# A gated-linear-attention recurrence on one NeuronCore: scores with exchanged operands in four column groups, and the small matmuls of a step in one block

## Chip, cores and metric

The kernel runs on one core of a Trainium2 chip. The metric is the device time of one launch in microseconds (us). The profile is of one execution; engines are named PE (TensorE matmuls), PEld (its weight loads), DVE (VectorE), ACT (ScalarE), POOL (GpSimd) and SP (the queue that issues the transfers).

## The reference, cut to what matters

Two layers run over 1024 prompt rows and 64 sample rows (8 sequences of 8). The second layer is gated linear attention with 4 heads, and the change lies in its recurrence:

```python
bcum = jnp.cumsum(lg, axis=3); blast = bcum[:, :, :, -1:]
q_dec   = q * jnp.exp(bcum)
k_intra = k * jnp.exp(-bcum)
k_state = k * jnp.exp(blast - bcum)
att = jnp.where(causal, jnp.einsum('nbhid,nbhjd->nbhij', q_dec, k_intra), 0.0)
o_intra = jnp.einsum('nbhij,nbhje->nbhie', att, v)
...
    o_inter = jnp.einsum('bhid,bhde->bhie', qc, s)
    s = dc[..., None] * s + jnp.einsum('bhjd,bhje->bhde', kc, vc)
```

Each head's output is then normalised, multiplied by a SiLU gate (`z`) and projected. The sample rows do the same with a state of their own, loaded and stored per sequence.

## The kernel before

Large products (`product_step`, the matmuls at L515) are made of a high and a low part: three passes (`w_hi` by `h_hi`, `w_hi` by `h_lo`, `w_lo` by `h_hi`) of three matmuls each, so nine matmuls per 128 rows of the contraction. Weights arrive in `stage` by SP, ACT copies the high part (`split_slot`, L317), POOL subtracts for the low part (`lo_slots`, L322).

The GLA layer loops over 4 heads. A head projects q, k, decay and v, turns v, runs the recurrence, and then the gate piece Z3, the row norms (NRM) and the output products. The gate pieces Z0, Z1 and Z2 (8 product steps each, 24 in all) are cut up by `fill(n)` and laid between the small matmuls of the recurrence, so that PE has work while the other engines prepare operands. `FILL_START` and `FILL_STEP` set how many stand before the loop and in each step.

The recurrence takes 128 prompt rows a step, 8 steps, and the loop has two more turns since the sample work trails by two. All engines are written out by hand and meet by semaphores. On PE, step `s` of the kernel before is:

- a fill of one product step; `scores(s+1)` (L1756, four matmuls with the 128 columns of `Kp[:, b]` stationary and 32 columns of `qd` moving, into `X[0]`); `key_rows(s+1)` (L1766, a transpose); `output(s)` (L1774 with the scores, L1782 with the state `S`); `update(s)` (L1791, the state's new term into `ps[1][:, 2]`)
- a fill of one product step; `mean_square(s-1)` (L1846, waits for POOL's `square_sum`); every second step `sample_inter` (L1811, waits for two sample states); `sample_update(s-2)` (L1823, L1824; waits for `ksm` of DVE's `ks_rows`)

After the loop's last turns come `sample_out` (L1833, L1838) and the last `sample_update`, then Z3. ACT in step `s` has: `gate_in` in steps 0 and 4 (the SiLU of a finished gate piece, which needs another activation table than Exp, L1140); `ksT_out(s+1)`; `exps(s+2)` (L1098 to L1105: `Kp`, `qd`, `ks`); `o_out(s)` (square and copy of the output); `exp_qs(s+1)`; `split_slot` in steps 1 and 5. POOL has `scale_kp(s+2)` (L881, `Kp` times the keys, without which no scores can start), `lo_slots` in steps 1 and 5, and `square_sum(s)` (L890, L892). DVE masks the scores into `att` (`att_out`, L1398, two buffers), scales `qd`, `ks`, `qs`, keeps the state (`state`, L1410), and has `ks_rows` (L1417, L1418) and `sample_state` (L1424) of the samples. SP loads a sample state into the place of the v rows that `update(s)` has read (`load_state`, L726).

Of the kernel before, what the change touches and what calls it, by code (L numbers as in the profile page):

```python
# [24 lines left out]
P = 128  # L25
# [5 lines left out]
KG = GW // P  # L31
TP = 1024
NB = 8
# [32 lines left out]

FILL_START, FILL_STEP = 7, 2

MINIS = 11

# [20 lines left out]
def trunk(nc, x_prompt, x_sample, c_prompt, c_sample, state_pool, state_gla, ada_w, ada_b, norm_g,  # L91
# [8 lines left out]
    with ctx:  # L100
# [128 lines left out]
        def sem(name):  # L229
            return ctx.enter_context(nc.semaphore(name))  # L230
# [43 lines left out]
        kp_zero, kp_exp, kp_ready = sem("kp_zero"), sem("kp_exp"), sem("kp_ready")  # L274
        qd_arg, qd_exp, qd_ready = sem("qd_arg"), sem("qd_exp"), sem("qd_ready")
        qs_exp, qs_ready, ks_exp, ks_ready = sem("qs_exp"), sem("qs_ready"), sem("ks_exp"), sem("ks_ready")
        att_done, att_ready, o_done, o_evac = sem("att_done"), sem("att_ready"), sem("o_done"), sem("o_evac")
        kT_done, ksT_ready, upd_done, S_ready = sem("kT_done"), sem("ksT_ready"), sem("upd_done"), sem("S_ready")
        smp_arg, smp_exp, smp_ready = sem("smp_arg"), sem("smp_exp"), sem("smp_ready")
# [636 lines left out]
        def _(act):  # L916
# [125 lines left out]
            def head(g, first):  # L1042
# [65 lines left out]
                def exp_qs(s):  # L1108
                    if s >= 1:
                        act.wait_ge(o_done, g * NSUP + s)  # L1110
                    nc.scalar.activation(qs[:], L[:, s * SUP:(s + 1) * SUP], ACT.Exp).then_inc(qs_exp, 1)

                def ksT_out(s):
                    act.wait_ge(kT_done, g * NSUP + s + 1)
                    if s >= 2:
                        act.wait_ge(upd_done, g * NSUP + s - 1)
                    nc.scalar.activation(ksT[:, s % 2, :], ps[1][:, 1, 0:P], ACT.Copy).then_inc(ksT_ready, 1)
# [31 lines left out]
                exp_qs(0)  # L1149
                act.wait_ge(smp_kT, g + 1)  # L1150
                nc.scalar.activation(ksT_s[:], ps[1][:, 1, 0:P], ACT.Copy).then_inc(smp_ksT, 1)
                ksT_out(0)
                exps(1)
                for s in range(NSUP):
                    if s in (0, 4):
                        gate_in(s // 4)
                    if s + 1 < NSUP:
                        ksT_out(s + 1)
                    if s + 2 < NSUP:
                        exps(s + 2)  # L1160
                    o_out(s)
                    if s + 1 < NSUP:
                        exp_qs(s + 1)
                    if s in (1, 5):
                        split_slot(L1, GP, act, g, GP.slot["Z2"] + s // 4)
                gate_in(2)
                act.wait_ge(smp_rows_done, g + 1)
                nc.scalar.activation(smp_rows, X[1], ACT.Copy).then_inc(smp_rows_out, 1)
                split_slot(L1, GP, act, g, GP.slot["O01"])
                o_out(NSUP)  # L1170

# [38 lines left out]
        def _(dve):  # L1210
# [134 lines left out]
            with dve.Fori(0, NG) as g:  # L1345
# [46 lines left out]

                def att_out(s):

                    if s >= 2:
                        wait_apart(dve, o_done, g * NSUP + s - 1)
                    wait_apart(dve, att_done, g * NSUP + s + 1)
                    nc.vector.copy_predicated(att[:, s % 2, :], causal[:], X[0][:, 0:P])\  # L1398
                        .then_inc(att_ready, 1)

                def state(s):
# [68 lines left out]
                qd_args(1)  # L1470
                scale_qk(1)
                for s in range(NSUP + 2):
                    if s >= 2:
                        ks_rows(s - 2)
                    if s + 1 < NSUP:
                        att_out(s + 1)
                    if s + 2 < NSUP:
                        qd_args(s + 2)
                        scale_qk(s + 2)
                    if s < NSUP:  # L1480
                        state(s)
                    if s + 1 < NSUP:
                        scale_qs(s + 1)
                    if s >= 2:
                        sample_state(s - 2)

                dve.wait_ge(s0_ready, (g + 1) * NB)
                dve.wait_ge(o_evac, (g + 1) * NSUP)
# [40 lines left out]
        def _(pe):  # L1529
# [179 lines left out]
            def head(g, first):  # L1709
# [38 lines left out]
                def scores(s):  # L1748
                    pe.wait_ge(kp_ready, g * NSUP + s + 1)
                    pe.wait_ge(qd_ready, g * NSUP + s + 1)  # L1750
                    if s >= 1:
                        pe.wait_ge(att_ready, g * NSUP + s)
                    else:
                        pe.wait_ge(smp_attr, g + 1)
                    for b in range(4):
                        last = nc.tensor.matmul(X[0][:, b * CH:(b + 1) * CH], Kp[:, b, :], qd[:, b * CH:(b + 1) * CH],  # L1756
                                                start=True, stop=True)
                    last.then_inc(att_done, 1)

                def key_rows(s):  # L1760
                    pe.wait_ge(ks_ready, g * NSUP + s + 1)
# [6 lines left out]
                def output(s):  # L1768
# [3 lines left out]
                        pe.wait_ge(o_evac, g * NSUP + s)  # L1772
                    for e in range(KG):
                        last = nc.tensor.matmul(ps[1][:, 0, e * P:(e + 1) * P], v[:, s, e * P:(e + 1) * P],  # L1774
                                                att[:, s % 2, :], start=(e == 0), stop=(s == 0 and e == KG - 1),
                                                skip_group_check=True)
                    if s:
                        pe.wait_ge(S_ready, g * NSUP + s)
# [7 lines left out]
                def update(s):  # L1786

                    pe.wait_ge(ksT_ready, g * NSUP + s + 1)
                    if s >= 3:
                        pe.wait_ge(s0_ready, g * NB + s - 2)  # L1790
                    nc.tensor.matmul(ps[1][:, 2, :], ksT[:, s % 2, :], v[:, s, :], start=True,  # L1791
                                     stop=True).then_inc(upd_done, 1)

# [22 lines left out]
                def sample_update(b):  # L1816

                    pe.wait_ge(ksm_ready, g * NB + b + 1)
                    if b + 2 < NSUP:
                        pe.wait_ge(S_ready, g * NSUP + b + 3)  # L1820
                    else:
                        pe.wait_ge(s0_ready, g * NB + b)
                    nc.tensor.matmul(ps[1][:, 2, :], ksm[:, 0, :], v_s[:], start=True, stop=False)  # L1823
                    nc.tensor.matmul(ps[1][:, 2, :], ksm[:, 1, :], v_s[:], start=False,  # L1824
                                     stop=True).then_inc(smp_upd, 1)
# [39 lines left out]
                fill(1)  # L1865
                scores(0)
                key_rows(0)
                fill(FILL_START - 5)
                for s in range(NSUP + 2):
                    if s <= NSUP:  # L1870
                        fill(1)
                    if s + 1 < NSUP:
                        scores(s + 1)
                        key_rows(s + 1)
                    if s < NSUP:
                        output(s)
                        update(s)
                        fill(FILL_STEP - 1)
                    if 1 <= s <= NSUP:
                        pe.wait_ge(att_ready, g * NSUP + min(s + 2, NSUP))  # L1880
                        mean_square(s - 1)
                    if s in (2, 4, 6, 8):
                        sample_inter(s - 2)
                    if s == NSUP + 1:
                        sample_out()
                    if s >= 2:
                        sample_update(s - 2)
                pe.sem_inc(L1.unit_done, 1)

                u = GP.unit["Z3"]  # L1890
# [61 lines left out]
```

## Time and profile before

| | us |
|---|---|
| median of 3 runs | 1720.27 |
| lowest and highest | 1717.53, 1724.99 |
| the profiled execution | 1722.27 |
| its span, first to last instruction | 1720.5 |
| PE busy | 1644.9 (96%) |
| DVE, ACT, POOL busy | 833.3, 483.5, 397.3 |
| mean granted TensorE clock | 0.98 of full speed |

The span is 1.8 us below the execution's own time, and that execution is 2.0 us above the median. A busy PE is not PE at its peak: ends of matmuls are modelled. The chain of waits counts each piece from the end of the one before it, so its durations add up to time.

### The profile page before, as it was taken

What the parts mean: (1) busy time and instruction counts of PE and PEld (TensorE: products, weight loads), DVE (VectorE), ACT (ScalarE), POOL (GpSimd) and SP (SyncE); (2) the same over time, 40 slices, a digit from 0 to 9 for tenths busy, and PEclk for the clock granted to TensorE, in tenths of its full rate; (3) what the DMA queues carried; (4) which work ended last, traced back from release to release, by engine and by line L of the source; (5) the groups of instructions that cost most, each with busy time, mean ns of one, the idle gap of its engine ahead of it and who ended that gap; (6) DMA issues with size and microseconds to landing.
All of it is one profiled execution on the core that took longest, in us unless ns stands there. A gap on an engine that the chain in (4) does not pass through costs nothing.

```text
span 1720.5 us, 26408 instructions
## 1 busy us (share of the span) xinstructions
PE 1644.9 (96%) x10307; PEld 1564.1 (91%) x10307; DVE 833.3 (48%) x1245; ACT 483.5 (28%) x1021; POOL 397.3 (23%) x392
## 2 busy tenths in 40 slices
PE   6899999999999999997999999999999999999997
PEld 3798999999999999996898899988999889998896
DVE  4494439453844475456224561235621456324465
ACT  4321112110211111134335403264132532225423
POOL 3221212121221212113224121232112331213310
PEclk8999999999999999997999999999999999999999
DMA  9322211221222122210112211122111221111212
GB/s 352 129 62 72 75 44 55 74 76 39 67 76 62 53 66 71 67 27 26 37 38 75 80 39 50 37 62 80 51 38 37 62 92 38 41 47 38 98 43 104
DMA packets 145621, 115.23 MB, mean 67 GB/s; under 512 B 5885, under 2 KB 128345, under 8 KB 145506
## 3 DMA queue, kind: packets, MB, share of 16 engines
q1 hardware_dynamic: 143680, 112.87, 21.3%
q8 instruction: 91, 1.49, 0.4%
q10 hardware_dynamic: 1834, 0.74, 0.2%
q14 instruction: 16, 0.13, 0.0%
HBM read 99.05 MB, written 15.00 MB: 66 GB/s over the span
## 4 chain that ended last, share of the span: by engine, by line
PE 88%; DVE 8%; ACT 2%; issue 1%; DMA 1%; SPq 0%; POOL 0%; ACTq 0%; DVEq 0%
PE psA L515 45%; PE psB L515 29%; PE psB L1774 2%; PE psB L1791 2%; PE psX L1756 2%; DVE PQ L1273 2%; PE psB L1782 1%; PE psX L1811 1%; DMA ada<-in_ada_w 1%; PE psB L1823 1%; DVE y_rows L1523 1%; PE psX L1636 1%; DVE a_hi L591 1%; ACT PQ L1049 1%; DVE ksm L1418 1%
## 5 line engine op out<-in xcount | busy, mean ns | idle before, releaser
L322 POOL TENSOR_TENSOR w_lo<-stage,w_hi 128x1024 fp32r<-128x1024 f32 x112 | 279.0, 2492 | 1059.4 <-ACT w_hi L317 1059.4
L515 PE MATMUL psA<-h_hi,w_hi 128*128 128x362 f32 (+1 forms) x1152 | 277.4, 350 | 24.5 <-DVE h_lo L453 15.3
L515 PE MATMUL psA<-h_lo,w_hi 128*128 128x362 f32 (+1 forms) x1152 | 256.9, 332 | 0.0
L515 PE MATMUL psA<-h_hi,w_lo 128*128 128x362 f32 (+1 forms) x1152 | 255.6, 330 | 0.0
L515 PEld LDWEIGHTS psA<-h_hi,w_hi 128*128 128x128 f32 x1152 | 202.4, 192 | 53.5 <-issue 48.3
L317 ACT ACTIVATE w_hi<-stage 128x1024 fp32r<-128x1024 f32 x112 | 120.1, 1072 | 392.3 <-PE psB L515 301.3
L515 PEld LDWEIGHTS psA<-h_lo,w_hi 128*128 128x128 f32 x1152 | 204.2, 193 | 0.0
L515 PEld LDWEIGHTS psA<-h_hi,w_lo 128*128 128x128 f32 x1152 | 203.4, 192 | 0.0
L515 PE MATMUL psB<-h_hi,w_hi 128*128 128x362 f32 (+1 forms) x576 | 129.1, 332 | 1.7 <-ACT kT L1049 1.7
L515 PE MATMUL psB<-h_hi,w_lo 128*128 128x362 f32 (+1 forms) x576 | 126.3, 327 | 0.0
L515 PE MATMUL psB<-h_lo,w_hi 128*128 128x362 f32 (+1 forms) x576 | 126.2, 327 | 0.0
L515 PE MATMUL psA<-a_hi,w_hi 128*128 128x362 f32 (+1 forms) x480 | 108.2, 333 | 5.9 <-DVE a_lo L594 5.9
L515 PE MATMUL psB<-a_hi,w_hi 128*128 128x362 f32 (+1 forms) x480 | 106.0, 329 | 4.2 <-DVE a_lo L1294 4.2
L515 PE MATMUL psA<-a_lo,w_hi 128*128 128x362 f32 (+1 forms) x480 | 105.7, 328 | 0.0
L515 PE MATMUL psB<-a_hi,w_lo 128*128 128x362 f32 (+1 forms) x480 | 105.6, 328 | 0.0
L515 PE MATMUL psA<-a_hi,w_lo 128*128 128x362 f32 (+1 forms) x480 | 105.3, 327 | 0.0
L515 PE MATMUL psB<-a_lo,w_hi 128*128 128x362 f32 (+1 forms) x480 | 105.3, 327 | 0.0
L515 PEld LDWEIGHTS psB<-h_hi,w_hi 128*128 128x128 f32 x576 | 98.3, 189 | 7.4 <-issue 6.3
L1273 DVE SCALAR_TENSOR_TENSOR PQ<-PQ,win_on 128x1220 f32<-128x1220 f32 (+2 forms) x48 | 103.2, 2150 | 2.8 <-DVE PQ L1268 0.5
L515 PEld LDWEIGHTS psB<-h_hi,w_lo 128*128 128x128 f32 x576 | 99.9, 188 | 0.0
L515 PEld LDWEIGHTS psB<-h_lo,w_hi 128*128 128x128 f32 x576 | 99.8, 188 | 0.0
L1364 DVE COPY v<-psB 128x512 f32<-128x512 f32 x32 | 20.6, 686 | 150.2 <-PE psB L1719 150.2
(314 smaller groups left out, 2369.7 us busy)
## 6 DMA issues: line engine op xcount, KB each, us to landing
stage<-in_gla_w_in SPq DMA_DIRECT2D x40, 512.0 KB, 3.9
stage<-in_pool_w_in SPq DMA_DIRECT2D x32, 512.0 KB, 4.1
ada_stage<-in_ada_w SPq DMA_DIRECT2D x24, 512.0 KB, 3.5
ada<-in_ada_w SPq DMA_DIRECT2D x8, 1024.0 KB, 12.2
stage<-in_pool_w_out SPq DMA_DIRECT2D x16, 512.0 KB, 3.5
v<-in_state_gla SPq DMA_DIRECT2D x32, 256.0 KB, 2.6
out_new_gla_sample<-v SPq DMA_DIRECT2D x32, 256.0 KB, 2.1
stage<-in_gla_w_out SPq DMA_DIRECT2D x16, 512.0 KB, 3.6
```

The source lines that it names most:

```text
L317: nc.scalar.activation(w_hi[:, j % 2, :], stage[:, j % 2, :], ACT.Copy).then_inc(lay.hi_done, 1)
L322: nc.gpsimd.tensor_tensor(w_lo[:, j % 2, :], stage[:, j % 2, :], w_hi[:, j % 2, :].bitcast(f32), ALU.subtract).then_inc(lay.lo_done, 1)
L515: last = nc.tensor.matmul(ps[u][:, t, 0:width], weight(w[:, p, :], k), a[:, k, n0:n0 + width], start=(k == 0 and pas == 0), stop=(k == kt ...
L591: nc.vector.tensor_copy(a_hi[:, i, :], oT[:, i, :]).then_inc(chain_v, 1)
L1049: last = nc.scalar.activation(dst[:, n0:n0 + w], ps[GP.set[u]][:, t, 0:w], ACT.Copy, scale=scale)
L1273: link(nc.vector.scalar_tensor_tensor(out=dst[:, lo:WE], in0=src[:, lo - sh:WE - sh], scalar=win_on[:].rearrange("p g k -> p (g k)")[:, ds ...
L1364: nc.vector.tensor_copy(v[:, 4 * half:4 * half + 4, i * P:(i + 1) * P], ps[1][:, half, :].rearrange("p (s n) -> p s n", s=4))
L1418: nc.vector.scalar_tensor_tensor(out=ksm[:, 1, :], in0=ksT_s[:], scalar=seq_rows[:, b:b + 1], in1=ksm[:, 0, :].bitcast(f32), op0=ALU.mult, ...
L1523: nc.vector.scalar_tensor_tensor(out=y_rows[0:n, s, :], in0=ps_y[s % 3][0:n].rearrange("p a n -> p (a n)"), scalar=y_rms[0:n, s:s + 1], in ...
L1756: last = nc.tensor.matmul(X[0][:, b * CH:(b + 1) * CH], Kp[:, b, :], qd[:, b * CH:(b + 1) * CH], start=True, stop=True)
L1774: last = nc.tensor.matmul(ps[1][:, 0, e * P:(e + 1) * P], v[:, s, e * P:(e + 1) * P], att[:, s % 2, :], start=(e == 0), stop=(s == 0 and e ...
L1791: nc.tensor.matmul(ps[1][:, 2, :], ksT[:, s % 2, :], v[:, s, :], start=True, stop=True).then_inc(upd_done, 1)
```

## The change

The scores' operands are exchanged: the 32 columns of `qd` of block `b` become the stationary operand and the 128 columns of `Kp[:, b]` the moving one, and the result of block `b` lies in partitions 32b to 32b+31 of `X[0]`, so each matmul uses another group of 32 columns of the array. The result is queries by keys, while `output` wants keys by queries. So ACT copies it to `att[:, 1]` (`scores_out`), PE turns it back into `X[0]` (`turn_scores`), and DVE masks it from there. `att` has one buffer left for the masked scores.

The order in the step is rewritten on PE, ACT and DVE, as the diff shows. PE has one block of small matmuls and then both product steps of fill; one product step moves from the start into the loop. `gate_in` moves from steps 0, 4 to 1, 5; the third one moves behind the copy of the sample rows. `update(s)` now waits for the `sample_state` of its own step.

```diff
-FILL_START, FILL_STEP = 7, 2
+FILL_START, FILL_STEP = 6, 2
+                def scores_out(s):
+                    act.wait_ge(att_done, g * NSUP + s + 1)
+                    if s >= 1:
+                        act.wait_ge(turn_done, g * NSUP + s)
+                    nc.scalar.activation(att[:, 1, :], X[0][:, 0:P], ACT.Copy).then_inc(score_out, 1)
...
+                scores_out(0)
                 ksT_out(0)
                 exps(1)
                 for s in range(NSUP):
-                    if s in (0, 4):
+                    if s + 1 < NSUP:
+                        scores_out(s + 1)
+                    if s in (1, 5):
                         gate_in(s // 4)
...
-                gate_in(2)
                 act.wait_ge(smp_rows_done, g + 1)
                 nc.scalar.activation(smp_rows, X[1], ACT.Copy).then_inc(smp_rows_out, 1)
+                gate_in(2)
...
-                    if s >= 2:
-                        wait_apart(dve, o_done, g * NSUP + s - 1)
-                    wait_apart(dve, att_done, g * NSUP + s + 1)
-                    nc.vector.copy_predicated(att[:, s % 2, :], causal[:], X[0][:, 0:P])\
+                    if s >= 1:
+                        wait_apart(dve, o_done, g * NSUP + s)
+                    wait_apart(dve, turn_done, g * NSUP + s + 1)
+                    nc.vector.copy_predicated(att[:, 0, :], causal[:], X[0][:, 0:P])\
...
                 for s in range(NSUP + 2):
+                    if s + 2 < NSUP:
+                        qd_args(s + 2)
                     if s >= 2:
-                        ks_rows(s - 2)
+                        sample_state(s - 2)
                     if s + 1 < NSUP:
                         att_out(s + 1)
                     if s + 2 < NSUP:
-                        qd_args(s + 2)
                         scale_qk(s + 2)
...
-                    if s >= 2:
-                        sample_state(s - 2)
+                    if 1 <= s <= NSUP:
+                        ks_rows(s - 1)
...
-                        last = nc.tensor.matmul(X[0][:, b * CH:(b + 1) * CH], Kp[:, b, :], qd[:, b * CH:(b + 1) * CH],
+                        last = nc.tensor.matmul(X[0][b * CH:(b + 1) * CH, 0:P], qd[:, b * CH:(b + 1) * CH], Kp[:, b, :],
...
+                def turn_scores(s):
+                    pe.wait_ge(score_out, g * NSUP + s + 1)
+                    nc.tensor.transpose(X[0][:, 0:P], att[:, 1, :], ident[:]).then_inc(turn_done, 1)
...
-                    if s >= 3:
-                        pe.wait_ge(s0_ready, g * NB + s - 2)
+                    if s >= 2:
+                        pe.wait_ge(s0_ready, g * NB + s - 1)
...
-                    if b + 2 < NSUP:
-                        pe.wait_ge(S_ready, g * NSUP + b + 3)
+                    if b + 2 <= NSUP:
+                        pe.wait_ge(S_ready, g * NSUP + b + 2)
...
                 fill(1)
                 scores(0)
                 key_rows(0)
+                turn_scores(0)
                 fill(FILL_START - 5)
                 for s in range(NSUP + 2):
-                    if s <= NSUP:
-                        fill(1)
                     if s + 1 < NSUP:
                         scores(s + 1)
                         key_rows(s + 1)
+                    if s in (2, 4, 6, 8):
+                        sample_inter(s - 2)
+                    if s >= 2:
+                        sample_update(s - 2)
                     if s < NSUP:
                         output(s)
+                    if 1 <= s <= NSUP:
+                        if s + 1 < NSUP:
+                            pe.wait_ge(score_out, g * NSUP + s + 2)
+                        else:
+                            pe.wait_ge(att_ready, (g + 1) * NSUP)
+                        mean_square(s - 1)
+                    if s + 1 < NSUP:
+                        turn_scores(s + 1)
+                    if s < NSUP:
                         update(s)
-                        fill(FILL_STEP - 1)
-                    if 1 <= s <= NSUP:
-                        pe.wait_ge(att_ready, g * NSUP + min(s + 2, NSUP))
-                        mean_square(s - 1)
-                    if s in (2, 4, 6, 8):
-                        sample_inter(s - 2)
                     if s == NSUP + 1:
                         sample_out()
-                    if s >= 2:
-                        sample_update(s - 2)
+                    if s <= NSUP:
+                        fill(FILL_STEP)
+                pe.wait_ge(L1.evac[0], evacs(GP, g, GP.unit["Z2"]))
                 pe.sem_inc(L1.unit_done, 1)
```

## Rows read from the trace of the kernel before

**Rows 1.** Who waited for whom, PE: total us, times, longest

```profile
PE psB L1823 <- DVE ksm L1418: 7.3, 4, 1.8
...
PE psA L515 <- DVE a_lo L594: 5.9, 4, 1.5
```

**Rows 2.** Chain of waits, second head's recurrence: start us, us, what

```profile
1122.26 0.81 PE psX L1756 x8
...
1148.30 0.34 PE psB L1823
1148.64 0.23 PE psB L1824
...
1151.18 0.14 PE psB L1766
1151.32 0.89 PE psB L1774 x8
...
1153.11 0.86 PE psB L1791 x2
...
1155.46 0.12 PE psX L1846 x2
1155.58 0.98 PE psX L1811 x4
...
1176.98 1.49 PE psA L515 x9
```

**Rows 3.** Chain of waits behind the last sample update, first and last head

```profile
964.51 0.79 PE psB L1823
...
965.73 3.86 PE psA L515 x18
...
1633.15 4.54 PE psA L515 x18
```

**Rows 4.** Stretches: length; busy PE, PEld, DVE, ACT, POOL; clock; DMA share, GB/s

```profile
200.00:206.00 6.00, 5.06 (x30) 5.06 (x31) 2.69 (x6) 0.00 (x0) 0.00 (x0) 1.00 0.25 87
...
1408.00:1411.00 3.00, 2.17 (x6) 1.97 (x7) 1.53 (x2) 1.09 (x1) 1.41 (x3) 0.50 0.03 5
```

**Rows 5.** Instructions of the tile ksm on DVE: ns min/median/max

```profile
L1418 DVE SCALAR_TENSOR_TENSOR ksm<-ksT_s,seq_rows,ksm x32: 350/353/2476, 911.3 to 1629.9; 128x128 fp32r<-128x128 f32 x32
```

**Rows 6.** Timeline of POOL, second head: start us, us, instruction

```profile
1126.09 1.45 POOL L881 TENSOR_TENSOR Kp<-Kp,kT 128x32 f32<-128x32 f32 x4 [5.54 <-ACT Kp L1098]
...
1133.02 2.38 POOL L322 TENSOR_TENSOR w_lo<-stage,w_hi 128x1024 fp32r<-128x1024 f32 x1 [1.39 <-ACT w_hi L317]
...
1136.17 0.45 POOL L892 TENSOR_TENSOR G<-G 128x128 f32<-128x128 f32 x1
...
1183.41 2.34 POOL L322 TENSOR_TENSOR w_lo<-stage,w_hi 128x1024 fp32r<-128x1024 f32 x1 [5.23 <-ACT w_hi L317]
```

**Rows 7.** Chain of waits, first layer: a matmul group in column groups, then 54 large matmuls

```profile
608.22 0.57 PE psX L1636 x16
608.79 9.14 PE psB L515 x54
```

**Rows 8.** Timeline of ACT, second head, from a gate piece on

```profile
1122.29 1.20 ACT L1140 ACTIVATE PQ<-psA 128x364 f32<-128x364 f32 x3 [1.49 <-PE psA L515]
1123.37 0.30 ACT L1117 ACTIVATE ksT<-psB 128x128 f32<-128x128 f32 x1
1123.68 1.28 ACT L1098 ACT_TABLE_LOAD   x1
...
1127.36 0.30 ACT L1111 ACTIVATE qs<-L 128x128 f32<-128x128 f32 x1
...
1131.89 1.06 ACT L317 ACTIVATE w_hi<-stage 128x1024 fp32r<-128x1024 f32 x1
```

**Rows 9.** Timeline of DVE, second head: the first masking in the loop

```profile
1123.17 0.30 DVE L1398 COPY_PREDICATED att<-causal,psX 128x128 f32<-128x128 int8 x1 [3.31 <-PE psX L1756]
```

**Rows 10.** Transfers of the tile v (sample states): us from issue to landing

```profile
DMA to landing us min/median/max: 2.0/2.6/3.8
```

More of the change, by code:

```diff
@@ L276, in trunk @@
         qs_exp, qs_ready, ks_exp, ks_ready = sem("qs_exp"), sem("qs_ready"), sem("ks_exp"), sem("ks_ready")
+        score_out, turn_done = sem("score_out"), sem("turn_done")
         att_done, att_ready, o_done, o_evac = sem("att_done"), sem("att_ready"), sem("o_done"), sem("o_evac")
@@ L1774, in output @@
                         last = nc.tensor.matmul(ps[1][:, 0, e * P:(e + 1) * P], v[:, s, e * P:(e + 1) * P],
-                                                att[:, s % 2, :], start=(e == 0), stop=(s == 0 and e == KG - 1),
+                                                att[:, 0, :], start=(e == 0), stop=(s == 0 and e == KG - 1),
                                                 skip_group_check=True)
```

## Prediction

> **What bounds the kernel now.** I read the page first: PE is busy for 96% of the span and nearly all of the chain that ended last is PE, so only what PE executes, what PE waits for, and its clock can move the time. Then the list of waits. Inside the GLA heads PE stands still for one thing that the change touches: the last sample update of each head waits 1.8 us for `ksm` of L1418, 7.3 us over four heads [rows 1]. The chain of waits gives what each small matmul group costs between two fills [rows 2]: scores 0.81, key transpose 0.14, each half of the output 0.89, update 0.86, mean square 0.12, the sample products of every second step 0.98, sample update 0.34 + 0.23, and a product step 1.49. A step of 0.81 + 0.14 + 2 x 0.89 + 0.86 + 0.12 + 0.57 + 2 x 1.49 is 7.26, or 8.24 with sample products, and PE has no gap in it. The other engines fit below that with room, except in the steps with `gate_in`.
>
> **The tail wait, removed.** `ks_rows(7)` stands behind two other DVE instructions there, and L1418 itself lasts 2.48 us instead of its usual 0.35 [rows 5], because POOL's `w_lo` started 0.02 us before it, at 1183.41, and holds it until it ends at 1185.75 [rows 6]. The page "SBUF — State Buffer" of the Trainium skill (the section on the diagram of ports) calls it an exclusive lock on a shared port pair, by which whoever starts first keeps it for the whole instruction; the trace agrees, with 2.48 for 0.35.
> In the changed order `ks_rows(7)` runs in turn 8, right after `sample_state(6)`, and PE has 3.0 us of fill before it wants the result. The wait goes: -7.3 us. What is late next is Z3, which needs `gate_in(2)`: its table load (1.28) can now run during the fill, its SiLU takes 1.1 to 1.2 [rows 8], and PE has the sample update (0.57) and `sample_out` (16 small matmuls from 1182.25 on, about 1.7) in front. So that is covered by 0.9 us.
> Behind that wait the clock is at its lower level: 0.50 is granted at 1408 to 1411 [rows 4], that is 1.2 of 2.4 GHz. The sample update then takes 0.79 + 0.43 rather than 0.57 in three heads of four, and the next 18 large matmuls 3.86, 4.07, 5.14 and 4.54 rather than 2.98 (the first and the last of four stand in [rows 3]). That is 5.7 + 2.1 = 7.8 us. PE had 1.7 us of small matmuls and then the idle 1.8 before it fell; waits of 1.5 us between large products left it at 1.00 [rows 1, 4]. With the wait gone I take the 7.8 as a gain.
>
> **The scores.** The same form, 128x32 weights and 128 moving columns in four column groups, is in the first layer at L1636. Sixteen of its passes take 0.57, and the 54 matmuls behind them 9.14 rather than 6 x 1.49 = 8.94, so 0.77 in all [rows 7]. Scores are 8 passes. Half of 0.57 with no cost of entering and leaving is 0.29, the lower end; 0.77, if all of it were fixed, is the upper. The form is the same and only the count halves, so I take 0.29 + 0.20 = 0.5. Against 0.81 that saves 0.31; the turn costs a transpose, 0.14 [rows 2]. Net -0.17 a step, 32 of them: -5.4 us (ends: -12 and +3).
> The page "TensorEngine Tiling (Array Packing)" (section Tiling Modes, key properties) speaks against this: a change of tiling mode drains the engine. The row agrees only in part, since 0.77 for sixteen passes is far below what they would take one by one; with no drain at all the step would save 0.38, with the whole 0.77 lost to it, it would lose 0.10.
> The rest of PE's work is the same, moved: fill 24 product steps, mean square, updates. Taking the mean square out from between two fills saves nothing that the chain shows.
>
> **New waits, step by step.** t = 0 is the start of `scores(s+1)`. Its results are ready at about 0.7: scores end at 0.5, and DVE's mask started within 0.1 to 0.25 of the end of the old ones (1123.07 to 1123.17 in the chain; a little earlier by issue) [rows 2, 9]. I add 0.06 for a semaphore.
> (1) Before the loop. `turn_scores(0)` follows `key_rows(0)` at once: it needs the copy (0.30), ready at 1.04, and PE is there at 0.64: wait 0.40. After it stands one product step instead of three before `scores(1)`, which need `Kp`. From the `ksT` copy to the end of POOL's `scale_kp` it is 0.2 + 1.1 + 1.45 = 2.7 without a table load [rows 6, 8], after the score copy: ready at 3.65. PE is there at 2.74: wait 0.91.
> (2) Step 1, `gate_in(0)`. In the kernel before the table load runs while ACT waits for PE. Now the score copy is in front of it and cannot start before 0.7, so the chain is copy 0.3, load 1.3, and from the SiLU's start (1122.29) to the end of `scale_kp` (1127.54) 5.25 [rows 6, 8]: `Kp` ready at 7.62. Step 1 has no sample work: 0.5 + 0.14 + 1.78 + 0.12 + 0.14 + 0.86 + 2.98 = 6.52. Wait 1.10 at `scores(3)`. The chain goes on: SiLU start to `exp_qs` 5.07, `split_slot` 0.2 later, `w_lo` 1.13 after that (1131.89 to 1133.02), and 3.60 until `square_sum(1)` is done (1136.62): 12.4. `mean_square(1)` now stands in the block, before the turn and the update, where PE would arrive at 6.52 + 4.06 = 10.6. So both waits together are 1.8. Before, a fill stood in between.
> (3) Step 5, `gate_in(1)`: the same chain, but the step is 0.57 longer: 0.55 + 0.68 = 1.23.
> (4) Z3: `mean_square(8)` after two product steps, 3.0. `split_slot(O01)` now comes after `gate_in(2)`, so POOL has 2.34 and then about 0.9 of sums: wait 0.45.
> (5) `sample_inter(6)` opens turn 8, 3.0 after `update(7)`; the state was issued 0.4 after that update and lands 2.6 later [rows 10]: wait 0.15. In turns 2, 4, 6 scores and keys (0.64) or an earlier wait cover it.
> In plain steps I find no wait. `update(s)` needs `sample_state(s-2)`: sample update ends at 1.2, DVE is done at 2.2, PE arrives at 3.2. The turn needs the copy at 1.0, PE arrives at 3.1. With one buffer, `att_out(s+1)` runs at 3.6, and `scale_qk`, `state`, `scale_qs` and `ks_rows` are queued behind it on DVE; they end near 6.2, with 7.1 to spare them. On ACT the score copy waits ahead of `exps`, which end at 2.9.
> A head: 0.40 + 0.91 + 1.8 + 1.23 + 0.45 + 0.15 = 4.94; four: +19.8 us.
>
> **The sum.** 1722.27 - 7.3 - 7.8 - 5.4 + 19.8 = 1721.6 on the profiled execution, which is 2.0 above the median of the runs: **1719.5**. The gain is real and the new waits eat it. The likeliest case is no change (below 0.5%, 8.6 us, a measurement of this kernel can hardly tell): chance 0.50, own range 1711 to 1729.
>
> **Rivals.**
> *The new waits do not show* (faster, 0.24). If ACT's chain in steps 1 and 5 is shorter by the 1.3 of the table load, because the load gets ahead of the score copy, (2) and (3) fall by 2.5 a head: 1709.5. If all of them go, 1700. For it: PE hides every such chain now. Against: in the trace the load stands directly before the first activation that needs it, behind a copy [rows 8].
> *The clock falls in the new waits* (slower, 0.11). A wait of 1.1 followed by a block of small matmuls and another of 0.7 is thinner work than the large products around the 1.5 us waits. At 1.9 us a time (7.8 over four), three such places a head would be +23: 1742; one of them, 1727. It decides from a wait near 1.8 on. Against: nothing below 1.8 did it [rows 1, 4].
> *The groups bring nothing* (0.13): scores stay near 0.8, as by the upper end: +9.3, 1729. This is half within 0.5% and half slower.
> *State loads late*: all of the 3.8 of the longest landing instead of 2.6 at four places a head is at most +15; chance 0.02. DVE instructions held by POOL's `w_lo` at about 8.7 in steps 1 and 5 would add some tenths.
>
> **Chances and range.** Faster is the first rival, and the low edge of the forecast's own spread adds little: 0.25. Slower is the clock, half of the third, and an underestimate of the waits (a semaphore or port held more, 0.5 us a gate step is 4 us): 0.24. Same: 0.51. The range, leaving out 2 in 10, is 1704 to 1732.
>
> **What would show it.** In the changed profile: L1823 waits for no `ksm` and the clock behind it is at 1.00; L1756 near 0.5 in the chain, a transpose line of 0.14 more; PE waiting for POOL `Kp` L881 about 2.5 us a head and for `square_sum` about 1.8; a wait of 0.4 for ACT's copy once a head. I am wrong if PE has no waits for POOL (then near 1702), if a clock below 1.00 shows inside the loop, or if L1756 stays near 0.8.

## The result

The changed kernel is slower: 1729.56 us (median of 5, 1725.84 to 1731.96) against 1721.89 us (median of 5, 1717.53 to 1724.99) for the kernel before. The ratio is 1.0051, 95% interval 1.0036 to 1.0067. The forecast of 1719.5 us, no change, was 10 us too low. The time lies inside the range of 1704 to 1732 that it gave, but the kernel is slower beyond the interval, and slower had a chance of 0.24.

The profiled execution took 1725.84 us, with a span of 1724.1 and PE busy for 1633.0 us (95%); before it was 1722.27, 1720.5 and 1644.9. So PE is busy for 11.9 us less, part of it because its clock is higher, and stands still longer. The lines of the changed kernel are numbered anew: `scores` is L1768, `key_rows` L1783, `turn_scores` L1775, `output` L1791 and L1799, `update` L1808, `sample_update` L1840 and L1841, `mean_square` L1863; `scale_kp` is L882, `square_sum` L891 and L893, the copy of the scores L1119, the second instruction of `ks_rows` L1429, `gate_in` L1148.

First the list of waits of the changed kernel, PE (us in total, times, longest). It answers to [rows 1]:

```profile
PE psX L1863 <- POOL G L893: 14.4, 12, 2.4
PE psX L1768 <- POOL Kp L882: 7.6, 12, 0.9
```

The wait for `ksm` is gone, 7.3 us, and two others stand there: 22.0 us. PE's timeline of the second head shows where (the bracket is the idle time before the instruction and what ended it):

```profile
1118.75 0.43 PE L1768 MATMUL psX<-Kp,qd 128*32 128x128 f32 x8 [0.87 <-POOL Kp L882]
1131.56 0.43 PE L1768 MATMUL psX<-Kp,qd 128*32 128x128 f32 x8 [0.72 <-POOL Kp L882]
1136.31 0.38 PE L1863 MATMUL psX<-ones,G 128*128 128x1 f32 x2 [0.64 <-POOL G L893]
1163.16 0.43 PE L1768 MATMUL psX<-Kp,qd 128*32 128x128 f32 x8 [0.30 <-POOL Kp L882]
1167.90 0.38 PE L1863 MATMUL psX<-ones,G 128*128 128x1 f32 x2 [0.63 <-POOL G L893]
1190.96 0.28 PE L1863 MATMUL psX<-ones,G 128*64 128x1 f32 x2 [2.27 <-POOL G L893]
```

These are the start, both gate steps (1 and 5), and Z3. The last is the largest by far, and it is there in all four heads. Together with the copy before `turn_scores(0)`, which the list of waits does not show as PE's (its weight load waits 0.33 us, taken below as 0.3), a head waits 5.8 us.

The chain of waits of the second head, which answers to [rows 2], gives the pieces of a step:

```profile
1140.70 0.36 PE psX L1768 x8
1141.05 0.26 PE psB L1783
1141.31 0.23 PE psB L1840
1141.54 0.23 PE psB L1841
1141.78 0.89 PE psB L1791 x8
1142.67 0.89 PE psB L1799 x8
1143.56 0.12 PE psX L1863 x2
1143.68 0.17 PE psX L1775
1143.85 0.86 PE psB L1808 x2
1144.71 2.98 PE psA L516 x18
1147.69 0.36 PE psX L1768 x8
```

Scores and key transpose are 0.62 where they were 0.95, and the turn costs 0.17. The step is 6.99 us where it was 7.28; one with sample products is 8.17 (from 1147.69) where it was 8.35 (the prediction's sum of pieces had 7.26 and 8.24). The key transpose, the first full-array matmul behind the groups, takes 0.26 instead of 0.14. With these 0.12 the eight passes and the transpose are still 0.33 below the old form. The page "TensorEngine Tiling (Array Packing)" of the Trainium skill (Tiling Modes, key properties) has the engine drain at each change of mode; the 0.12 agree with it, and bound what leaving the groups costs here.

The clock, in stretches of the changed kernel (length; busy PE, PEld, DVE, ACT, POOL; granted clock; DMA share, GB/s), which answers to [rows 4]:

```profile
1190.00:1193.00 3.00, 2.04 (x13) 2.02 (x14) 1.98 (x4) 1.73 (x4) 0.91 (x1) 1.00 0.49 158
1408.00:1411.00 3.00, 3.00 (x26) 3.00 (x25) 0.96 (x2) 2.85 (x7) 1.19 (x1) 1.00 0.25 92
1640.00:1643.00 3.00, 3.00 (x11) 3.00 (x11) 3.00 (x4) 1.59 (x2) 0.00 (x0) 0.50 0.00 0
```

The columns of busy time are as in [rows 4]. At 1408 the clock is at 1.00, the upper level of 2.4 GHz, where it had been at 0.50. But in the fourth head it is at 0.50 (1.2 GHz) behind the new wait in Z3. In the stretch of the GLA layer (850 to 1700), the time lost at the lower level, added up over windows of 2 us as length times what the granted clock lacks of 1.00, was 8.5 us before and is 1.7 in this execution. The mean granted clock of this execution is 0.984; in the other four it is 0.979 to 0.984, and their spans are longer by 2 to 6 us.

### The profile page after: what moved, and what is told of

It reads as the page before. It is cut to its first block, busy times and chain, and to the rows that moved or that the text cites. A ratio compares the mean times of both kernels' runs of the same rounds, so it can differ in the third digit from the quotient of the medians.

```text
span 1724.1 us, 26543 instructions
## 1 busy us (share of the span) xinstructions
PE 1633.0 (95%) x10339; PEld 1533.9 (89%) x10339; DVE 829.9 (48%) x1245; ACT 490.2 (28%) x1053; POOL 403.4 (23%) x392
## 4 chain that ended last, share of the span: by engine, by line
PE 54%; issue 26%; POOL 9%; DVE 6%; ACT 3%; DMA 1%; SPq 0%; POOLq 0%; ACTq 0%; DVEq 0%
PE psA L516 26%; PE psB L516 21%; POOL w_lo L323 5%; DVE PQ L1284 1%; POOL Kp L882 1%; POOL G L891 1%; DMA ada<-in_ada_w 1%; PE psB L1808 1%; POOL G L893 1%; PE psB L1791 1%; DVE y_rows L1535 1%; PE psX L1648 1%; DVE a_hi L592 1%; PE psB L1799 1%; ACT h_hi L483 0%
## 5 line engine op out<-in xcount | busy, mean ns | idle before, releaser
L516 PE MATMUL psA<-h_hi,w_hi 128*128 128x362 f32 (+1 forms) x1152 | 273.9, 346 | 24.7 <-DVE h_lo L454 15.3
```

What stands on the lines that cost most here:

```text
L516: last = nc.tensor.matmul(ps[u][:, t, 0:width], weight(w[:, p, :], k), a[:, k, n0:n0 + width], start=(k == 0 and pas == 0), stop=(k == kt ...
```

## Why Z3's mean square is late

POOL's timeline in the changed kernel, second head:

```profile
1185.72 2.40 POOL L323 TENSOR_TENSOR w_lo<-stage,w_hi 128x1024 fp32r<-128x1024 f32 x1 [9.11 <-ACT w_hi L318]
1188.07 1.51 POOL L891 TENSOR_TENSOR G<-G 128x128 f32<-128x128 f32 x1
1189.66 1.25 POOL L893 TENSOR_TENSOR G<-G 128x64 f32<-128x64 f32 x1
```

and DVE's beside it:

```profile
1186.70 4.03 DVE L1443 SCALAR_TENSOR_TENSOR oT<-oT,vecT,PQ 128x1088 f32<-128x1088 f32 x2 [1.99 <-ACT oT L1138]
```

`square_sum(8)` stands behind `w_lo`, as forecast, and should then take some 0.9 us. It takes 2.8, because DVE's gate products of Z0 and Z1 run at the same time. They read two operands from SBUF, as `w_lo` and the sums do. The two products of this head take 2.57 and 1.54 where the shortest of the kernel is 1.35:

```profile
L1443 DVE SCALAR_TENSOR_TENSOR oT<-oT,vecT,PQ x12: 1351/1538/2645, 963.6 to 1651.2; 128x1088 f32<-128x1088 f32 x12
...
L1443 DVE SCALAR_TENSOR_TENSOR oT<-oT,vecT,PQ x2: 1540/2052/2565, 1186.7 to 1189.2; 128x1088 f32<-128x1088 f32 x2
```

The times fit engines that take turns. The first product starts at 1186.70, while `w_lo` runs, and ends 1.15 us after `w_lo` does; the first sum, 0.46 by itself, ends 0.3 us after that product; the second product ends 1.15 us after the first sum, and the second sum, 0.32 by itself, ends 0.2 us after the second product.

In the run "scores and tail" below, which has the sums ahead of `w_lo` and of the gate products, the same two take 0.46 and 0.32. DVE has only a `sample_state` beside them, which reads one operand from PSUM:

```profile
1179.88 0.46 POOL L891 TENSOR_TENSOR G<-G 128x128 f32<-128x128 f32 x1 [6.53 <-ACT G L1137]
1180.42 0.32 POOL L893 TENSOR_TENSOR G<-G 128x64 f32<-128x64 f32 x1
1181.11 3.52 POOL L323 TENSOR_TENSOR w_lo<-stage,w_hi 128x1024 fp32r<-128x1024 f32 x1 [0.36 <-ACT w_hi L318]
```

There it is `w_lo` that meets the gate products, 3.52 for 2.4, and nobody waits for it. The run "sums first" has a case in between: the first sum ends 0.01 us before the first gate product starts and takes 0.46, the second starts 0.07 us behind that product and takes 1.47, while the product, which was first, takes no more than 1.42:

```profile
1197.31 1.47 POOL L893 TENSOR_TENSOR G<-G 128x64 f32<-128x64 f32 x1
```

This is the rule that the forecast took from the Trainium skill ("SBUF — State Buffer", the section on the diagram of ports: who starts first keeps the shared pair for the whole instruction), seen from POOL's side, and the trace agrees, with 1.51 for 0.46. The forecast did not ask at term (4) who would hold POOL; "a semaphore or port held more" stands only among its chances for slower, at 0.5 us a gate step.

## The experiments

Ratios are to runs of the kernel before taken with them (medians 1719.74, 1720.93 and 1720.59 us in the three groups of runs), with 95% intervals; a ratio is not exactly the quotient of the two medians. A head is counted from the first matmul of `sample_scores` to the first of the row norms, in the profiled execution:

| kernel | median us | ratio | the four heads, us |
|---|---|---|---|
| before | | 1 | 85.63, 85.83, 86.93, 85.81 |
| changed | 1729.56 | 1.0051 [1.0036, 1.0067] | 87.33, 87.13, 87.16, 88.70 |
| late square | 1719.91 | 0.9999 [0.9990, 1.0008] | 84.92, 84.79, 84.79, 84.79 |
| old form | 1738.89 | 1.0104 [1.0089, 1.0118] | 91.35, 89.54, 91.07, 91.10 |
| order alone | 1730.22 | 1.0058 [1.0044, 1.0072] | 86.68, 89.75, 88.12, 88.28 |
| order, late square | 1720.81 | 1.0000 [0.9987, 1.0012] | 84.19, 85.80, 84.18, 84.21 |
| scores alone | 1715.30 | 0.9966 [0.9954, 0.9979] | 82.70, 84.30, 85.36, 82.71 |
| tail alone | 1708.89 | 0.9926 [0.9908, 0.9943] | 82.24, 82.26, 82.26, 82.25 |
| scores and tail | 1702.17 | 0.9884 [0.9868, 0.9899] | 80.77, 80.80, 80.75, 80.80 |
| sums first | 1740.32 | 1.0106 [1.0090, 1.0121] | 89.92, 91.63, 91.59, 91.64 |
| gate late | 1731.69 | 1.0066 [1.0051, 1.0080] | 87.75, 88.97, 88.92, 87.44 |
| all waits | 1714.41 | 0.9960 [0.9947, 0.9973] | 83.38, 83.53, 83.53, 83.53 |

**Late square.** The changed kernel with Z3's mean square two product steps later:

```diff
-                    if k == 1:
+                    if k == 3:
                         pe.wait_ge(smp_o_evac, g + 1)
                         mean_square(NSUP)
```

> The changed kernel with one edit: the mean square of the sample rows stands two product steps later inside Z3. In the changed kernel PE waits 2.3 us for it in each head, and the clock falls behind it in some. My theory, that this wait and not the waits for Kp and w_lo is what I mis-sized: the wait of 2.3 us goes, 9.2 us and a clock loss of 1.5 to 6 with it, so 1719 us or a little less, ratio to before 0.997 to 1.000. Rival, the time comes from something else (a clock loss from the waits inside the loop, or the first layer): it stays at 1726 to 1730, ratio 1.004.

Measured 1719.91 us, 9.7 below the changed kernel. The waits, as us in total, times, longest:

```profile
PE psX L1768 <- POOL Kp L882: 7.5, 12, 0.9
PE psX L1863 <- POOL G L893: 5.3, 8, 0.7
PE psA L516 <- ACT PQ L1148: 1.8, 4, 0.5
```

Of 14.4 us for the sums 5.3 are left, those of the gate steps; 1.8 us come back as a wait of the first output product for Z3's own `gate_in`. The clock is at 1.00 behind Z3's mean square in all heads. The four heads are 11.0 us shorter, and the 1.8 stand behind them. So one wait, with the clock behind it, is worth nearly the 10 us of the miss. That the kernel lands where the forecast had it is partly luck: the other misses, listed below, nearly cancel.

**Old form.** The changed kernel with the operands exchanged back; the turn stays, so that `output` gets the scores transposed and the prompt's output is wrong; it is here for its time alone:

```diff
-                        last = nc.tensor.matmul(X[0][b * CH:(b + 1) * CH, 0:P], qd[:, b * CH:(b + 1) * CH], Kp[:, b, :],
+                        last = nc.tensor.matmul(X[0][:, b * CH:(b + 1) * CH], Kp[:, b, :], qd[:, b * CH:(b + 1) * CH],
```

> The changed kernel with the operands of the scores as before (Kp stationary with 128 columns, one column group), copy and turn kept; its attention matrix is therefore transposed wrongly, so it leaves the prompt's scores wrong and is only there for its time. My theory, that the four groups do save what the chain shows (0.36 + 0.26 for scores and key transpose against 0.81 + 0.14): 0.25 to 0.33 us more per step, 32 of them, 8 to 10 us over the changed kernel, 1738 us, ratio 1.009 to 1.011. Rival, the groups bring nothing because entering and leaving them drains PE: it stays at 1729, ratio 1.005.

Measured 1738.89, 9.3 above the changed kernel: the four column groups do save, and "the groups bring nothing" falls.

**Order alone.** The new order of PE, ACT and DVE with the old scores, no copy and no turn, and two buffers of `att` again:

```diff
-                    wait_apart(dve, turn_done, g * NSUP + s + 1)
+                    wait_apart(dve, att_done, g * NSUP + s + 1)
...
-                            pe.wait_ge(score_out, g * NSUP + s + 2)
+                            pe.wait_ge(att_ready, g * NSUP + s + 2)
...
-                    if s + 1 < NSUP:
-                        turn_scores(s + 1)
```

> The order of the changed kernel with the scores of the kernel before: no exchange, no copy, no turn, two buffers for the masked scores. My theory, that the waits in the steps with a gate piece come from the score copy standing before the table load: no wait for Kp in steps 2 and 6 and none for the sums of steps 1 and 5; the wait before step 0 (1.3 us) and the one of 2.3 us in Z3 stay, the one for ksm is gone. That is 1.8 + 1.9 less and 3.6 more a head against before: 1720 to 1724, ratio 0.999 to 1.001. Rival, the order in one block is itself what costs: 1727 or more.

Measured 1730.22, on the rival's side. The waits are those expected, one at the start and one in Z3 of each head, and none in the gate steps. The missed part is for the larger share the clock (6.8 us at the lower level, none expected): in the second head it falls behind a wait of 1.29 us, in the scores, output and update and the first product step after it, and again behind Z3's wait. The rest is some 0.65 us a head of which more below. PE's timeline and the stretches behind the waits (columns as above):

```profile
1119.56 1.08 PE L1765 MATMUL psX<-qd,Kp 128*128 128x32 f32 x8 [1.29 <-POOL Kp L882]
1192.52 0.28 PE L1860 MATMUL psX<-ones,G 128*64 128x1 f32 x2 [2.28 <-POOL G L893]
```

```profile
1120.00:1126.00 6.00, 6.00 (x29) 4.97 (x29) 2.16 (x7) 4.12 (x11) 2.58 (x6) 0.72 0.11 42
1192.00:1196.00 4.00, 3.48 (x13) 3.46 (x14) 2.98 (x6) 2.41 (x4) 0.47 (x1) 0.60 0.17 60
```

The first kind happened in one head of four, the second in three.

**Order, late square.** The same with the mean square at `k == 3`.

> The changed order with the old scores (as in the run of the order alone), and the last mean square after four product steps of Z3 instead of two. That run had 9.2 us of waits for the sums in Z3 and lost about 5 us of clock behind them in three heads, and 5.2 us of waits for Kp at the start, with the clock down behind one of four. If these are all that the order costs, this comes to 1714 to 1718, ratio 0.996 to 0.999, with the 5.2 us of Kp waits left. Rival: the order is slow in itself, the block of small matmuls being thin work behind which the clock falls in more heads than one; then the Kp waits or other places show granted clocks of 0.5 and the time stays at 1722 or more, ratio above 1.001.

Measured 1720.81, 9.4 less, though 1714 to 1718 was expected. The heads gave what was counted on: 338.4 us for the four instead of 352.8. Outside them stand the 0.5 us for Z3's `gate_in` once a head, and in the profiled execution more time lost to the clock ahead of the recurrence (the first head starts 3.4 us later than in the order alone); whether that holds for the other executions no trace shows. It has 5.1 us of waits for `Kp` left, and the clock falls behind the one in the second head again. By the medians the order, freed of its wait in Z3, gains nothing: it takes away a wait of 7.3 us and its clock, and pays with others. In the profiled executions its heads are 5.8 us shorter than those of the kernel before, and 1.8 of that goes to the `gate_in` behind them; why the medians show none of the other 4 is open.

**Scores alone.** The order of before with the exchanged operands, the copy, and the turn between `output` and `update`:

```diff
                     if s < NSUP:
                         output(s)
+                        if s + 1 < NSUP:
+                            turn_scores(s + 1)
                         update(s)
```

> The order of the kernel before with the new scores: exchange, copy and turn (between output and update), one buffer for the masked scores, qd_args ahead of the masking. My theory: 0.2 us less a step, 6 us in all, less 0.2 to 0.5 us of new waits a head, the tail wait of 1.8 us with its clock loss as before: 1716 to 1718, ratio 0.997. Rival, the turn and the copy cost what the groups save: 1721, ratio 1.000. Second rival, masking waits so long on DVE that other operands are late: PE waits inside the steps and 1725 or more.

Measured 1715.30, a ratio of 0.9966: 4.4 us gained between the medians without the block, a little more than expected, since no new wait is in the list. The wait for `ksm` stays at 7.3 us, with the clock behind it in two heads.

**Tail alone.** The kernel before, with nothing of the change:

```diff
 POOL
+                    square_sum(s)
                     if s == 1:
                         lo_slots(L1, GP, pool, g, GP.slot["Z2"])
...
-                    square_sum(s)
 ACT
+                o_out(NSUP)
                 split_slot(L1, GP, act, g, GP.slot["O01"])
-                o_out(NSUP)
```

> The kernel before with two edits and nothing of the change: POOL does its square sums ahead of the subtraction for the low part, and ACT copies the last output out ahead of the high part of O01. My theory is that the removed tail wait is worth 7.3 us and the clock behind it about 7 more, and that both come from any edit that frees the last ksm, so this needs neither the block nor the exchanged operands: waits for ksm gone, clock at 1.00 behind the last sample update, ratio about 0.991 to the kernel before (0.989 to 0.993), about 14 to 16 us off. It should also add up with the 5 to 6 us that the exchanged operands gave in the order of before. Rival: the clock falls in the tail anyhow, since sample_out's small matmuls are thin work; then only the 7.3 us come, ratio 0.995 to 0.997. Second rival: sums ahead of the low part make DVE's instructions late at another place, as they did in the changed order; then there is a new wait of 2 us at the sample update and the ratio is near 1.00 or above.

Measured 1708.89, a ratio of 0.9926, in the expected range, though the 11.7 us between the medians are less than the 14 to 16 expected. PE waits for no `ksm`, and the clock is at 1.00 behind the last sample update in each head. The four heads are 15.2 us shorter than before in the profiled executions: the 7.3 of the wait, and 7.9 that fit the clock behind it. The profiled execution before is 1.7 us above its median in this group, so that its 15.2 may be more than is usual. So what the new order was meant for is to be had by moving two calls. Which of the two does it was not tried.

**Scores and tail.** Both together.

> The order of the kernel before with the new scores (as in e4) and its tail mended without the block: on POOL the sums stand before w_lo, on ACT the samples' output is squared before the split of O01, so w_lo cannot hold L1418. My theory: the wait of 1.8 us and the clock loss behind it go, 3.7 us a head less than e4: 1700 to 1703, ratio 0.989. Rival, the wait stays because ks_rows(7) is behind sample_state(6) anyway: 1712.

Measured 1702.17, ratio 0.9884, the fastest of all and faster than both kernels by 19 and 27 us. No wait is left in the recurrence. The heads are 1.47 us shorter on average than those of the tail alone, 5.9 us over four, 0.18 a step: this is the worth of the exchanged operands, copy and turn included, with nothing else in play. The chain of waits, one step:

```profile
1146.17 0.35 PE psX L1768 x8
1146.53 0.26 PE psB L1783
1146.79 0.89 PE psB L1791 x8
1147.68 0.89 PE psB L1799 x8
1148.58 0.11 PE psX L1775
1148.69 0.86 PE psB L1808 x2
```

**Sums first.** The changed kernel with POOL's `square_sum(s)` ahead of `lo_slots`, as in the tail alone.

> The changed kernel with one edit on POOL: square_sum(s) stands before lo_slots in steps 1, 5 and 8. My theory, that the three waits for sums come from w_lo queued before them (and in Z3 from the DVE products that then hold POOL): the waits of 0.64, 0.63 and 2.3 us go, 3.6 us a head, 14 us, and the clock losses in Z3 with them: 1712 to 1716 us against 1729, ratio to before 0.995 to 0.997. Rival, the sums are late because ACT squares late, so POOL's order brings little: 1726 or more. Second rival, w_lo comes too late for the fills then: new waits for w_lo, 1720.

Measured 1740.32 where 1712 to 1716 was expected. The waits for the sums are gone, and a larger one is there:

```profile
PE psB L1840 <- DVE ksm L1429: 16.1, 8, 2.0
```

POOL's and DVE's timelines in step 1 of the second head:

```profile
1136.41 2.34 POOL L323 TENSOR_TENSOR w_lo<-stage,w_hi 128x1024 fp32r<-128x1024 f32 x1
```

```profile
1136.57 2.33 DVE L1429 SCALAR_TENSOR_TENSOR ksm<-ksT_s,seq_rows,ksm 128x128 fp32r<-128x128 f32 x1
```

With the sums ahead of it, `w_lo` starts 0.16 us before `ks_rows` and holds it for 2.33 us instead of 0.35, the same collision as at the tail of the kernel before [rows 5, 6], now twice a head. In the changed order two product steps, the next scores and the sample products stand between `ks_rows(0)` and its use. Each wait, up to 2.01 us long, is followed by a stretch at the lower clock: 18.8 us lost in this execution. The same edit is part of the 12 us that the tail alone gains in the one order, and costs 11 in the other.

**Gate late.** The changed kernel with ACT's `gate_in` behind `exps`, and DVE's `ks_rows` ahead of `scale_qs`.

```diff
-                    if s in (1, 5):
-                        gate_in(s // 4)
                     if s + 1 < NSUP:
                         ksT_out(s + 1)
                     if s + 2 < NSUP:
                         exps(s + 2)
+                    if s in (1, 5):
+                        gate_in(s // 4)
...
```

> The changed kernel with gate_in behind exps in ACT's order (steps 1 and 5), and ks_rows ahead of scale_qs on DVE. My theory: the waits for Kp in steps 2 and 6 (0.72 and 0.30) go, but w_hi, w_lo and the sums behind them start no earlier, so PE waits as long as before at the mean square: 1.4 and 0.9 instead of 0.64 and 0.63. Z3's wait stays. 1728 to 1731, ratio 1.004 to 1.006. Rival, the Kp waits were a cost of their own and 1.0 a head is won: 1725, ratio 1.002.

Measured 1731.69, within the error of the changed kernel. The waits in both gate steps went, those for the sums too, which were expected to grow (for `Kp` 3.5 us are left, at the start, and 9.2 for the sums, in Z3), and another took their place, the fill for ACT: the next gate piece can't be filled until `gate_in` has read the last out of its set.

```profile
PE psA L516 <- ACT PQ L1148: 9.4, 8, 1.4
```

**All waits.** Sums first, gate late, `ks_rows` early, the late square, and `FILL_START` at 7, with one product step ahead of `turn_scores(0)` and one instead of two in step 0.

> The changed kernel with every wait in it addressed: POOL's sums before w_lo, gate_in behind exps, ks_rows ahead of scale_qs, the samples' mean square at the fourth product step of Z3, seven product steps before the loop with one of them between key transpose and turn, and one in step 0. My theory: no wait is left in the recurrence, 5.8 us a head less than the changed kernel and no clock loss: 1702 to 1706, ratio 0.990 to 0.992. Rival, the waits come back elsewhere since ACT, DVE and POOL have no room in a step of 7 us: 1712 or more.

Measured 1714.41 where 1702 to 1706 was expected. No small matmul waits for anything. PE's timeline of the second head has three waits, all for `gate_in`, and the list of waits sums them to 11.2 us:

```profile
1125.66 0.76 PE L516 MATMUL psA<-h_hi,w_hi 128*128 128x364 f32 x3 [1.42 <-ACT PQ L1148]
1157.20 0.76 PE L516 MATMUL psA<-h_hi,w_hi 128*128 128x364 f32 x3 [0.96 <-ACT PQ L1148]
1196.66 0.76 PE L516 MATMUL psA<-a_hi,w_hi 128*128 128x364 f32 x3 [0.50 <-ACT PQ L1148]
```

In the changed order `gate_in` is squeezed from both sides: early it delays `Kp` and the sums, late it delays the fill. None of the edits tried in that order reached the order of before with two calls moved.

## Why the prediction was wrong

Step by step, on the profiled execution. The four heads were forecast to be 0.7 us shorter and are 6.1 longer.

- **The tail wait**: right, -7.3 us, and so was its cause, as the tail alone shows.
- **The clock behind it**: forecast -7.8; it is gone, but 1.7 us came back behind Z3's wait, net -6.8.
- **The scores**: forecast -5.4 us. By themselves they give -5.9 (scores and tail against tail alone). The price taken between the two ends was right within 0.02 us a step.
- **Terms (1), (2), (3)**: forecast 0.40 + 0.91, 1.8 and 1.23 a head; the list of waits has 0.3 + 0.87, 0.72 + 0.64 and 0.30 + 0.63. Places, releasers and order are as forecast, and the sizes look 0.1 to 0.4 too high. But the list holds only PE's idle time, and a wait costs more than that. From the second half of the output to the turn PE takes 1.95 us with the wait of 0.64 in it, and 1.03 in the next step, without one:

```profile
1134.61 1.06 PE L1799 MATMUL psB<-qs,S 128*128 128x128 f32 x8
...
1136.56 0.31 PE L1775 MATMUL psX<-ident,att 128*128 128x128 f32 x1
...
1142.51 1.06 PE L1799 MATMUL psB<-qs,S 128*128 128x128 f32 x8
...
1143.54 0.31 PE L1775 MATMUL psX<-ident,att 128*128 128x128 f32 x1
```

  The idle time is counted from the end of the output, 1.06 behind its start, but without a wait the mean square starts 0.89 behind that start: this overlap of 0.17 is lost, and the mean square takes 0.25 to the turn instead of 0.14. From one `scores` to the next, a step with sample products is 8.17, and 9.07 with this wait, so it costs 0.90; the one of 0.30 costs 0.37 (7.37 for 7.00), and the one of 0.72 costs 0.80 (7.37, against 6.57 for the same step in the scores and tail). By this (2) is 1.7 for 1.8 and (3) 1.27 for 1.23. The load of the activation table stands behind the copy of the scores, so the first rival falls:

```profile
1124.68 0.28 ACT L1119 ACTIVATE att<-psX 128x128 f32<-128x128 f32 x1 [2.38 <-PE psX L1768]
1124.98 1.28 ACT L1148 ACT_TABLE_LOAD   x1
1126.28 1.20 ACT L1148 ACTIVATE PQ<-psA 128x364 f32<-128x364 f32 x3
```

- **Term (4), the failed step**: "POOL has 2.34 and then about 0.9 of sums: wait 0.45". Measured 2.27 to 2.4 in each of four heads. The 2.34 was right, at 2.40; the 0.9 was 2.8, because two gate products of DVE were running. The forecast had used the same row, 2.48 for 0.35, to price the wait that it removed, and then took an undisturbed duration for the next two-operand instructions on the same pair of engines. That is some +7.5 us, and the late square undoes it: -9.7 with what the clock adds.
- **Term (5)**, 0.15 a head: no wait for a sample state is in the list. The 3.8 us of [rows 10], which the rival of late loads took as the longest landing, is a store: those rows hold both directions, and the 32 loads by themselves landed after 2.5 to 2.8.
- **What no term held**: the work in the heads, with waits and clock taken out, shrank by 3.0 us and not by 5.4 (6.1 = -7.3 - 6.8 + 23.2 - 3.0, the 23.2 being 7.6 + 14.4 and 1.2 for `turn_scores(0)`). What the waits cost beyond the list, 0.26 twice and 0.07 once a head by the steps above, is 2.4 us, and so about the whole of that difference. The order has something of the kind too: without the wait in Z3, 84.19 - 1.28 of wait is 82.9 a head, against 82.25 for the tail alone. The starts of the matmuls in the third head of both say where these 0.65 stand: 0.26 around the wait of 1.28 at the start, beyond its idle time, 0.10 in each of the two steps with sample products between the scores (8.45 for 8.35), none in the plain steps, and about 0.2 behind the last scores. Why the same matmuls take longer in the last two is open.

Together: 3.4 for the waits (+7.5 for term (4), -4.1 for the rest), 2.4 for the work, which is mostly what waits cost beyond the list, and 1.0 for the clock make the 6.8 us by which the heads are above the forecast. The profiled execution is only 4.2 above the 1721.6 that was forecast for it, since it is 2.6 us shorter than the one before outside the heads (its first head starts 3.2 us earlier), where the code is the same: that is luck. It is also better than the median of its kernel: 1729.56 is another 3.7 up, and the mean clock of three of the other four executions is lower, but no trace of them shows in which places. With the 2.1 by which the forecast went below 1721.6 for the median, 6.8 - 2.6 + 3.7 + 2.1 is the 10 us.

"The clock falls in the new waits" was written for the gate steps and from 1.8 us on. It came true in Z3, where the wait is 2.3 us, in one head of four here and three of four in the order alone; and it did not need the 1.8 of the forecast, since it fell once behind 1.29 us.

## What to carry to other kernels

When an edit moves an instruction of DVE or POOL with two operands in SBUF, look at what the other engine does at the new time and price the instruction held as well as free; a free duration is only the lower end. Before rewriting an order to remove a wait, try what is late in the old one: here two calls moved on POOL and ACT gave all that the new order was for, at none of its waits. And a wait among small matmuls costs its idle time, here 0.1 to 0.3 us beyond that, and in some heads as much again in clock.

## What was not expected of the hardware

- **Two engines holding each other in turn.** POOL's sums took 1.51 for 0.46 and 1.25 for 0.32, and DVE's two gate products 4.03 for twice 1.35, while they overlapped; beside the products `w_lo` took 3.52 for 2.4. In all these cases both engines read two operands from SBUF.
- **The clock behind equal waits.** Z3's wait of 2.3 us brought the lower level in one head of four in the changed kernel's profile and in three of four in the order alone; one of four starts with 1.29 us did. The same row does not always have the same price.
- **A wait costs more than its idle time.** PE idle for 0.64 us ahead of the mean square made the step 0.90 longer; of the excess, 0.17 is the overlap of two matmuls that the wait takes away, and 0.11 a slower start behind it.
- **The same code at another clock.** Ahead of the recurrence (0 to 850 us), where all kernels are alike, the profiled executions lost between 20.4 us (late square) and 29.0 us (scores and tail) at the lower level, added up over windows of 2 us. The first head starts at 889.27 in the one and at 894.50 in the other. Differences of that size between single executions say nothing of an edit. The medians do, and within one execution the heads, if the clock in them is counted apart.
